# Hybrid attention and expert layer on one core: the end rebuilt, with weighted sums on TensorE and the last expert's tile added by a 0/1 matrix

## The chip, the cores and the metric

The kernel runs on one core of one Trainium2 chip. A core has five engines that work side by side: TensorE (PE in the profile; its weight loads are PEld), VectorE (DVE), ScalarE (ACT), GpSimd (POOL) and SyncE (SP), which here only issues transfers. They meet through semaphores. SBUF is the working memory with 128 partitions, PSUM the memory of 8 banks (512 f32 per partition each) into which TensorE writes. The metric is the device time of one execution in microseconds (us).

## The reference, cut to what matters

One layer on 128 context tokens (x_prompt) and 512 latent tokens (x_sample), width 1024: modulation from c, attention and a gated spatial mixer side by side, an output projection, then a mixture of 32 experts of which each token uses two. Around each half stands a norm, and its gated result is added to the residual. All of it is f32.

```python
x = x + gate1 * _rms_norm(mix, g_post_mix)
h2 = _rms_norm(x, g_pre_ffn) * (1 + scale2) + shift2
# _hier_moe: softmax over 4 groups, best group; in it the best two of 8 experts
weights = jax.nn.softmax(e_top, axis=-1) * g_top          # two weights per token
hid = silu(t @ w_gate[e]) * (t @ w_up[e])                 # per expert, 1024 -> 256
f = sum over the token's two experts of weight * (hid @ w_down[e])
x = x + gate2 * _rms_norm(f, g_post_ffn)                  # outputs y_prompt, y_sample
```

## The kernel before

The 640 tokens are 5 tiles of 128 (tile 0 is the context, cond_of(i) picks its gate). Each engine has its own program, written out by hand; the order of work is the order of the lines in it, and semaphores tie the programs together. No planner is at work.

**Up to the experts.** Modulation, input projection (L600, L619), spatial mixer, attention (20 steps of head pairs), output projection (L722) and, tile by tile beside it, residual, second norm and router. SP writes the gates to DRAM (L453) and reads them back broadcast (L455). After attention POOL reloads the residual into res (L1661, L1662). The router's result is turned into row numbers: src_row says which half rows of h2 an expert's tile gathers, dst_row where its results go. Two consecutive partition halves hold the two 512-wide halves of 64 rows (SLOT = 64), so one tile serves 64 assignments of an expert. Where an expert has more, extra tiles follow; extra_at[e] and extra_at[e+1] are the first and the end of expert e's extra tiles. With these inputs there are three.

**One expert e** (weights of 3 MB, six places: four ring slots, w_5, w_6):
- POOL gathers its rows from DRAM (gather), SP has loaded w_gate, w_up, w_down (load_expert, L436, L438).
- TensorE transposes them (next_x, L520), VectorE copies them to xt (copy_x, L1358).
- TensorE: products with w_gate and w_up (products, gate_up, L869), ScalarE SiLU (silu, L1572), VectorE times the up part (hidden, L1365).
- TensorE transposes hid (L520), ScalarE copies it (L1582), TensorE: product with w_down (down, L877), ScalarE copies the result to a y buffer (L1586), POOL scatters it to expert_results in DRAM (scatter, L1699). There are three y buffers.
- Then every engine loads extra_at[e] and extra_at[e+1] into registers and, if there are extra tiles, loops over them with the same weights (TensorE L914 to L926, VectorE L1374 to L1380, ScalarE L1587 to L1596, POOL extras, L1711). The loop waits for each step of its own tile.

Experts 0 to 25 run with the products of e+1 ahead of the down product of e. From expert 26 on (is_late, the part written out after the loop) an engine finishes e, its extra tiles included, and only then takes the next: TensorE does next_x(e+2), then products(e+1) (L928 to L931); VectorE copy_x(e+2), then hidden(e+1).

**The end.** SP waits for the scatters of all 32 experts and for the extra tiles' (L506, L507) and issues five reads of 1 MB, one per token tile: y_back[:, i] holds both experts' results of the 128 tokens. Per tile then: ScalarE y_sum = y_back[0] x w_tok[0] (L1606), VectorE y_sum += y_back[1] x w_tok[1] (L1397), ScalarE the squares with their sum (L1615), VectorE mean plus EPS (L1407), POOL to the power -1/2 (L1628), VectorE times that and the gate (L1410), VectorE plus residual (L1412), SP store (L513). VectorE's order is weighted(i+1), mean(i), then the last two steps of tile i-1:

```python
for i in range(TILES + 1):
    if i + 1 < TILES: weighted(i + 1)
    if i < TILES: ...          # waits for f_sq, mean of tile i
    if i: ...                  # waits for f_rs, the two last steps of tile i - 1
```

## Time and profile before

| | |
|---|---|
| median of 3 runs | 674.7 us (673.72 to 675.25) |
| the profiled execution's own time | 672.75 us |
| its span, first to last instruction | 671.0 us |
| PE busy | 548.3 us (82%) |
| DVE, ACT, POOL busy | 192.8, 151.3, 173.5 us |
| chain that ended last | PE 54%, DMA 26%, DVE 8%, ACT 4% |
| mean DMA rate over the span | 254 GB/s |

The page cuts the span into 40 slices of 16.8 us; a digit is the busy share in tenths:

```
PE   0479999999987789999997899789899998878788700
DMA  8999108054199300620044959999999999999183
```

Busy times are sums per engine. The chain is followed back from the last instruction, at each step to what released it, and so shows what sets the time; in the timeline the bracket behind a row is the engine's idle time ahead of it and what ended it. "issue" is time in which the engine waited for nothing that the profile shows. Times in the trace count from the start of the span.

### The profile page before, as it was taken

How to read it: one execution, taken by the hardware profiler on the slowest of the kernel's cores; microseconds unless marked ns; L12 is line 12 of the kernel's file. 1: busy time of each engine (PE TensorE's matmuls, PEld its weight loads, DVE VectorE, ACT ScalarE, POOL GpSimd, SP SyncE). 2: the span in 40 equal slices, each digit the busy share in tenths (PEclk: the TensorE clock that was granted, in tenths of full speed). 3: DMA queues.
4: the chain of work that ended last, by engine and by line, in shares of the span. 5: the costliest groups of instructions: out<-in, count | busy, mean ns of one | idle time of the engine just before them, and what ended most of it. 6: DMA issues, size and time to landing. Idle time of an engine off the chain costs nothing.

```text
span 671.0 us, 9726 instructions
## 1 busy us (share of the span) xinstructions
PE 548.3 (82%) x3055; PEld 301.5 (45%) x3056; DVE 192.8 (29%) x575; ACT 151.3 (23%) x375; POOL 173.5 (26%) x240
## 2 busy tenths in 40 slices
PE   0479999999987789999997789899998878788700
PEld 0235654444354455455554445455554444444300
DVE  1150312001367763244467102011111111111037
ACT  2630102002126663232221011111111111111142
POOL 1000000002513332143335423334332222221212
PEclk9999999999998999999998899999998898899955
DMA  8999108054199300620044959999999999999183
GB/s 254 401 404 397 65 1 312 1 193 183 37 312 409 124 2 1 219 95 31 33 166 143 409 220 407 395 392 408 405 395 401 402 404 393 406 403 395 47 327 157
DMA packets 53192, 170.23 MB, mean 254 GB/s; under 512 B 7660, under 2 KB 8340, under 8 KB 52256
## 3 DMA queue, kind: packets, MB, share of 16 engines
q1 hardware_dynamic: 46112, 155.45, 60.1%
q0 software_dynamic: 6752, 14.13, 5.9%
q8 instruction: 23, 0.38, 0.2%
q10 hardware_dynamic: 288, 0.13, 0.1%
q14 instruction: 17, 0.14, 0.1%
HBM read 163.23 MB, written 14.58 MB: 265 GB/s over the span
## 4 chain that ended last, share of the span: by engine, by line
PE 54%; DMA 26%; DVE 8%; ACT 4%; SPq 3%; issue 3%; PEld 1%; PEldq 0%; POOL 0%; ACTq 0%; POOLq 0%; DVEq 0%
DMA ring<-in_w_down_dram 12%; PE ps L722 10%; PE ps L619 10%; PE ps L869 8%; PE ps L600 5%; PE ps L520 5%; DMA w<-in_w_down_dram 5%; DMA ring<-in_w_mod_dram 4%; PE ps L877 4%; PE ps L601 3%; PE ps L699 2%; PE ps L539 2%; DMA ring<-in_w_up_dram 2%; ACT probs L1495 2%; DVE probs L1130 1%
## 5 line engine op out<-in xcount | busy, mean ns | idle before, releaser
L869 PE MATMUL ps<-ring,xt 128*64 128x256 f32 x768 | 97.3, 410 | 19.9 <-DMA ring<-in_w_up_dram 12.3
L869 PEld LDWEIGHTS ps<-ring,xt 128*64 128x64 f32 x768 | 64.7, 148 | 58.6 <-issue 36.6
L619 PE MATMUL ps<-ring,h_t 128*128 128x512 f32 x160 | 69.5, 594 | 0.0
L1365 DVE TENSOR_TENSOR hid<-act_g,ps 128x128 f32<-128x128 f32 x32 | 9.2, 287 | 185.7 <-ACT act_g L1572 185.7
L722 PE MATMUL ps<-ring,mix_t 128*128 128x512 f32 x120 | 53.6, 596 | 0.0
L1699 POOL DMA_INDIRECT expert_results<-y_sb,idx_out x32 | 32.7, 1023 | 58.3 <-ACT y_sb L1586 55.4
L619 PEld LDWEIGHTS ps<-ring,h_t 128*128 128x128 f32 x160 | 30.1, 190 | 37.6 <-issue 37.6
L869 PE MATMUL ps<-w,xt 128*64 128x256 f32 x352 | 40.4, 382 | 6.0 <-DMA w<-in_w_up_dram 4.1
L877 PE MATMUL ps<-ring,hid_t 128*64 128x512 f32 x176 | 42.6, 605 | 3.2 <-ACT hid_t L1582 2.6
L600 PE MATMUL ps<-ring,h_t 128*128 128x512 f32 x80 | 42.0, 607 | 2.7 <-DVE h_t L1022 2.7
L1628 POOL TENSOR_TENSOR gm_stats<-gm_stats,half_pow 128x8 f32<-128x8 f32 x5 | 9.7, 1939 | 129.5 <-DVE gm_stats L1088 129.5
L1688 POOL DMA_INDIRECT xg<-h_rows,idx_in x32 | 33.4, 1045 | 30.7 <-POOL idx_in L1685 24.3
L1572 ACT ACTIVATE act_g<-ps 128x128 f32<-128x128 f32 x32 | 8.9, 278 | 139.7 <-PE ps L869 139.7
L869 PEld LDWEIGHTS ps<-w,xt 128*64 128x64 f32 x352 | 27.8, 137 | 21.1 <-issue 12.0
L539 PE MATMUL ps<-ring,cond 128*32 128x384 f32 x256 | 23.9, 518 | 14.7 <-DMA ring<-in_w_mod_dram 14.7
L1656 POOL TENSOR_SCALAR probs<-probs,att_stats 128x384 f32<-128x384 f32 (+2 forms) x40 | 23.0, 589 | 48.1 <-DVE att_stats L1144 48.1
L1586 ACT COPY y_sb<-ps 128x512 f32<-128x512 f32 x32 | 18.8, 586 | 68.0 <-PE ps L877 68.0
L722 PEld LDWEIGHTS ps<-ring,mix_t 128*128 128x128 f32 x120 | 22.2, 190 | 25.8 <-issue 25.7
L1628 POOL TENSOR_TENSOR stats<-stats,half_pow 128x1 f32<-128x1 f32 (+1 forms) x16 | 13.4, 837 | 75.4 <-DVE stats L1188 39.5
L1358 DVE COPY xt<-ps 128x512 f32<-128x512 f32 x32 | 22.1, 691 | 22.7 <-PE ps L520 20.4
L520 PE MATMUL ps<-cst,probs 128*128 128x128 f32 x120 | 19.9, 289 | 10.4 <-ACT p_t L1505 9.0
L1685 POOL COPY idx_in<-src_row 128x1 uint32 (+1 forms) x29 | 6.5, 225 | 78.6 <-PE ps L520 78.5
(238 smaller groups left out, 725.5 us busy)
## 6 DMA issues: line engine op xcount, KB each, us to landing
ring<-in_w_mod_dram SPq DMA_DIRECT2D x8, 3072.0 KB, 20.2
ring<-in_w_gate_dram SPq DMA_DIRECT2D x22, 1024.0 KB, 9.3
ring<-in_w_up_dram SPq DMA_DIRECT2D x22, 1024.0 KB, 13.7
ring<-in_w_down_dram SPq DMA_DIRECT2D x22, 1024.0 KB, 16.0
w<-in_w_gate_dram SPq DMA_DIRECT2D x10, 1024.0 KB, 8.6
w<-in_w_up_dram SPq DMA_DIRECT2D x10, 1024.0 KB, 13.6
w<-in_w_down_dram SPq DMA_DIRECT2D x5, 1024.0 KB
w_6d<-in_w_down_dram SPq DMA_DIRECT2D x5, 1024.0 KB, 16.2
```

The costliest lines, as they stand in the source:

```text
L520: return pe.matmul(out, in_, ident[0:n_in, 0:n_in], is_transpose=True, start=True, stop=True)
L539: last = pe.matmul(ps[32 * g:32 * g + 32, hh, 0:MB // 2], cond[:, k, :], w[:, k, hh * (MB // 2):(hh + 1) * (MB // 2)], start=(k < 4), stop ...
L600: pe.matmul(ps[:, 4 + 2 * (i % 2), 0:ATT], h, w[:, k, 0:ATT], start=(k == 0), stop=(k == KC - 1))
L619: last = pe.matmul(ps[:, 4 + u % 4, :], h_t[:, k, i * P:(i + 1) * P], w[:, k, :], start=(k == 0), stop=(k == KC - 1))
L722: last = pe.matmul(ps[:, 2 * (i % 2) + hh, :], mix_t[:, k, i * P:(i + 1) * P], rhs, start=(k == 0), stop=(k == KC - 1))
L869: last = pe.matmul(bank[fh * SLOT:(fh + 1) * SLOT, 0:FE].rearrange("p (a f) -> p a f", a=2), x_t[:, k % 4, (k // 4) * SLOT:(k // 4 + 1) * ...
L877: last = pe.matmul(bank[ch * SLOT:(ch + 1) * SLOT, :], h[:, fh * SLOT:(fh + 1) * SLOT], w[:, fh, ch * 512:(ch + 1) * 512], start=(fh == 0) ...
L1358: dve.tensor_copy(xt[:, c % 2].rearrange("p c s -> p (c s)"), ps[:, c % 2, :]).then_inc(x_cp, 1)
L1628: pool.tensor_tensor(dst, src, half_pow[:, 0:n], ALU.pow).then_inc(done, 1)
L1656: last = pool.tensor_scalar(p, p, att_stats[:, INV, t, a:a + 1], 1.0, ALU.mult, ALU.mult)
L1688: pool.indirect_dma_start(xg[:, j, :], None, h2_halves, bass.IndirectOffsetOnAxis(ap=idx_in[:, j, 0:1], axis=0), bounds_check=2 * TILES * ...
L1699: pool.indirect_dma_start(y_halves, bass.IndirectOffsetOnAxis(ap=idx_out[:, c, 0:1], axis=0), y_buf(c), None, bounds_check=2 * TOPK * TILE ...
```

## The change

It has five parts.

1. **End.** The two weighted sums of a tile go to TensorE. w_diag[:, i, k] is the identity times w_tok (one 128x128 matrix per tile and choice), and per tile and 512-wide half three products add up in one PSUM bank: w_diag x y_back of choice 0, the same of choice 1, and sel_last x y_l, which adds the last expert's rows. ScalarE squares straight from PSUM, VectorE's step with the gate reads PSUM. y_back now lies in ring slots 2 and 3, y_out, junk_3 and gate_f where w_5 and w_6 were. Four pairs of banks turn; tile 4 waits for tile 0's output.
2. **Last expert (LAST = 31).** It isn't scattered. Its result is copied with a scale of w_last, the weight that belongs to each of its rows, and sel_last[:, i] has a 1 where a row of its tile belongs to a token of tile i. Since its rows of expert_results are read and never written now, SP zeroes all of expert_results in attention (five writes of 1 MB from a tile of zeros that POOL sets), and POOL's reload of the residual waits for them. w_last comes from a small table of weights in DRAM that POOL writes and gathers ahead of scatter 26. SP's wait before the five reads covers the scatters of experts 0 to 30 and the extra tiles'.
3. **Extra tiles of the last expert** are looked for after those of expert 30 and before the last expert's own products, on TensorE, VectorE and ScalarE; TensorE waits there for the last expert's weights.
4. **Late order.** From expert 26 on TensorE does products(e+1), then next_x(e+2), and VectorE hidden(e+1), then copy_x(e+2).
5. select_last() on VectorE makes w_diag and sel_last after the copy_x of expert 31, in expert 29's step; three small steps for w_pair and w_last follow the extra rows. Two semaphores (ws_raw and gmn_bc in, xg_x zeroed) are merged with others.

```diff
@@ sync: after the gates, and before the five reads @@
+            sp.wait_ge(zeros_made, 1)
+            for i in range(TILES):
+                sp.dma_start(y_dram[i * P:(i + 1) * P].rearrange("t k (h n) -> t (k h) n", n=512),
+                             zeros[:].unsqueeze(1).broadcast_to((P, 2 * TOPK, 512))).then_inc(s_gate, 16)
...
-            sp.wait_ge(rows_made, ALL_ROWS)
-            sp.dma_start(gate_bc[:, 1], gates_dram[1:2].broadcast_to((P, 2, D))).then_inc(gate_in, 16)
+            sp.wait_ge(y_mm, LAST - 1)
+            sp.wait_ge(expert_done, LAST - 1)
+            sp.dma_start(gate_f[:], gates_dram[1:2].broadcast_to((P, 2, D))).then_inc(gate_in, 16)
             for i in range(XS):
-                sp.wait_ge(y_st[i], 16 * len(range(i, EXPERTS, XS)))
+                sp.wait_ge(y_st[i], 16 * len(range(i, LAST, XS)))
...
@@ tensor, expert(q, c), after down(...) @@
+                if not below(e, LAST) and isinstance(e, int):
+                    return
+                extras(q, c, xb, e + 1)
+                pe.sem_inc(expert_done, 1)
+                if isinstance(e, int) and e + 1 == LAST:
+                    extras(*nth(q, c, 1), xb, LAST - 1)
+                if late and e + 1 < EXPERTS:
+                    products(*nth(q, c, 1))
+                if late and e + 2 < EXPERTS:
+                    next_x(*nth(q, c, 2))
+
+            def extras(q, c, xb, y_read):
+                e = q * WS + c
+                wgu, wd = weights(c)
+                if isinstance(e, int) and e == LAST:
+                    pe.wait_ge(wgu_in[c % LS], 32 * loads(q, c))
+                    pe.wait_ge(wd_in[c % LS], 16 * loads(q, c))
                 lo = pe.value_load(extra_at[0:1, bass.ds(e, 1)], min_val=0, max_val=MAX_EXTRA)
                 hi = pe.value_load(extra_at[0:1, bass.ds(e + 1, 1)], min_val=0, max_val=MAX_EXTRA)
                 with pe.If(lo < hi), pe.Fori(lo, hi) as x:
...
@@ tensor, after all_experts @@
+            y_l = y_buf(LAST % WS)
+            pe.wait_ge(y_cp, EXPERTS)
+            pe.wait_ge(rows_made, LAST_SEL)
+            for i in range(TILES):
+                pe.wait_ge(back_in[i], 16)
+                if i >= 4:
+                    pe.wait_ge(f_sq, i - 3)
+                    pe.wait_ge(f_out, i - 3)
+                for h in range(2):
+                    cut_, bank = slice(512 * h, 512 * (h + 1)), ps[:, 2 * (i % 4) + h, :]
+                    rows_ = slice(SLOT * h, SLOT * (h + 1))
+                    for k in range(TOPK):
+                        pe.matmul(bank, w_diag[:, i, k, :], y_back[:, i, k, cut_], start=(k == 0), stop=False)
+                    last = pe.matmul(bank, sel_last[rows_, i, :], y_l[rows_, :], start=False, stop=True)
+                last.then_inc(f_sum, 1)
...
@@ vector, expert(q, c) @@
+                extras(q, c, xb)
+                if isinstance(e, int) and e + 1 == LAST:
+                    extras(*nth(q, c, 1), xb)
+                if late and e + 1 < EXPERTS:
+                    hidden(*nth(q, c, 1))
+                if late and e + 2 < EXPERTS:
+                    copy_x(*nth(q, c, 2))
+                if isinstance(e, int) and e + 2 == LAST:
+                    select_last()
...
+            def select_last():
+                dve.tensor_copy(iota[:, 0:SLOT], const("slot")[:, 0:SLOT])
+                link(dve.tensor_scalar(iota[:, SLOT:P], const("slot")[:, 0:SLOT], float(SLOT), None, ALU.add))
+                link(dve.tensor_scalar(tok_l[:], dst_row[:, LAST:LAST + 1], 2, None, ALU.logical_shift_right))
+                link(dve.tensor_copy(tok_f[:, 0:1], tok_l[:]))
+                for i in range(1, TILES):
+                    last = dve.tensor_scalar(tok_f[:, i:i + 1], tok_f[:, 0:1], float(P * i), None, ALU.subtract)
+                link(last)
+                for i in range(TILES):
+                    for k in range(TOPK):
+                        dve.tensor_scalar(w_diag[:, i, k, :], ident, w_tok[:, i, k:k + 1], None, ALU.mult)
+                    last = dve.tensor_scalar(sel_last[:, i, :], iota[:], tok_f[:, i:i + 1], None, ALU.is_equal)
+                last.then_inc(rows_made, 1)
...
@@ vector, end: weighted(i) is gone, the rest keeps its order @@
+                    link(dve.scalar_tensor_tensor(y_out[:, i - 1].rearrange("p (h n) -> p h n", h=2), y_ps(i - 1),
+                                                  stats[:, 7, i - 1:i],
+                                                  gate_f[:, cond_of(i - 1), :].rearrange("p (h n) -> p h n", h=2),
+                                                  ALU.mult, ALU.mult))
+                    dve.tensor_tensor(y_out[:, i - 1], res[:, i - 1], y_out[:, i - 1], ALU.add).then_inc(f_out, 1)
...
@@ scalar, expert 31's copy @@
+                    act.wait_ge(wl_in, 16 + 16)
+                    act.activation(y_buf(c), ps[:, 5 + c % 2, :], ACT.Copy, scale=w_last[:, 0:1]).then_inc(y_cp, 1)
+                    return
...
@@ gpsimd, expert 26, ahead of its scatter @@
+                    pool.wait_ge(rows_made, WEIGHTS)
+                    pool.dma_start(w_dram.rearrange("(i p r) o -> p i (r o)", p=P, i=TILES),
+                                   w_pair[:].rearrange("p i k h -> p i (k h)")).then_inc(wl_in, 16)
+                    pool.tensor_copy(idx_l[:, 0:1], dst_row[:, LAST:LAST + 1]).then_inc(out_idx, 1)
+                    pool.wait_ge(wl_in, 16)
+                    pool.wait_ge(out_idx, e + 1)
+                    pool.indirect_dma_start(w_last[:, 0:1], None, w_dram,
+                                            bass.IndirectOffsetOnAxis(ap=idx_l[:, 0:1], axis=0),
+                                            bounds_check=2 * TOPK * TILES * P - 1, oob_is_err=False).then_inc(wl_in, 16)
```

## Rows read from the trace of the kernel before

**Rows 1.** Chain that ended last, 618 to 672 us: start, us, what
```profile
628.55 0.51 issue
629.06 3.69 PE ps L869 x32
...
636.09 0.59 ACT y_sb L1586
...
637.53 2.67 DMA expert_results<-y_sb,idx_out
...
641.11 8.91 DMA y_back<-expert_results
...
666.20 1.23 DVE y_out L1412
```

**Rows 2.** Timeline, experts 29 and 30: start, us, engine line op, idle before
```profile
612.38 3.67 PE L869 MATMUL ps<-ring,xt 128*64 128x256 f32 x32
...
616.41 0.29 DVE L1365 TENSOR_TENSOR hid<-act_g,ps 128x128 f32<-128x128 f32 x1 [3.23 <-ACT act_g L1572]
...
619.30 0.75 PE L520 MATMUL ps<-cst,xg_x 128*128 128x128 f32 x4
...
620.09 0.69 DVE L1378 COPY xt<-ps 128x512 f32<-128x512 f32 x1 [3.39 <-PE ps L520]
...
620.83 3.67 PE L869 MATMUL ps<-ring,xt 128*64 128x256 f32 x32 [0.78 <-DVE xt L1378]
```

**Rows 3.** Timeline of one issue on SP; DMA views of w_up's landings
```profile
597.89 0.46 SPq L436 DMA_DIRECT2D ring<-in_w_up_dram  x1
...
w<-in_w_up_dram SPq DMA_DIRECT2D x1, 1024.0 KB, 14.8
...
ring<-in_w_up_dram SPq DMA_DIRECT2D x1, 1024.0 KB, 13.1
```

**Rows 4.** DMA view, first 12 us: KB each, us to landing
```profile
v_all<-in_cache_v_dram POOLq DMA_DIRECT2D x1, 64.0 KB, 3.3
...
w_r<-in_router_group_dram POOLq DMA_DIRECT2D x1, 16.0 KB, 4.4
```

**Rows 5.** Chain, 40 to 50 us: VectorE steps
```profile
45.38 0.18 DVE pre L996
...
45.88 1.38 DVE h_t L1022 x5
```

**Rows 6.** Timeline of TensorE: gate and up products of three experts
```profile
508.83 5.36 PE L869 MATMUL ps<-ring,xt 128*64 128x256 f32 x32 [2.37 <-DMA ring<-in_w_up_dram]
...
551.46 3.67 PE L869 MATMUL ps<-w,xt 128*64 128x256 f32 x32 [2.34 <-DMA w<-in_w_up_dram]
...
576.88 5.36 PE L869 MATMUL ps<-ring,xt 128*64 128x256 f32 x32 [2.06 <-DMA ring<-in_w_up_dram]
```

**Rows 7.** Lines 914 and 927, 601 to 605 us: ns min/median/max, start
```profile
L914 PEldq TENSOR_LOAD <-extra_at x1: 314/314/314, 602.2 to 602.2; - x1
...
L927 PEldq EVENT_SEMAPHORE  x1: 51/51/51, 603.8 to 603.8; - x1
```

**Rows 8.** Chain, 100 to 160 us; groups by form of weight loads
```profile
113.40 27.47 PE ps L619 x64
...
L619 PEld LDWEIGHTS ps<-ring,h_t 128*128 128x128 f32 x160 | 30.1, 190 | 37.6 <-issue 37.6
```

**Rows 9.** Timeline of the end
```profile
640.26 2.56 SPq L509 DMA_DIRECT2D y_back<-expert_results  x5
645.08 1.15 ACT L1606 ACTIVATE y_sum<-y_back,w_tok 128x1024 f32<-128x1024 f32 x1 [8.40 <-DMA y_back<-expert_results]
...
659.97 1.06 ACT L1615 ACTIVATE junk<-y_sum 128x1024 f32<-128x1024 f32 x1 [2.29 <-DVE y_sum L1397]
...
662.37 0.14 DVE L1407 TENSOR_SCALAR stats<-stats 128x1 f32<-128x1 f32 x1
```

**Rows 10.** Windows, attention: engines' busy us, clock, DMA share, GB/s
```profile
230.00:240.00 10.00, 8.75 (x69) 5.19 (x65) 6.81 (x27) 4.78 (x15) 2.73 (x4) 1.00 0.00 0
```

More of the change, by code:

```diff
@@ L48 @@
 LOOPED = (EXPERTS - 2 - WS) // WS
+LAST = EXPERTS - 1
 MB = 768
@@ L1596, in expert @@
                     act.copy(y_x[:, :], ps[:, 5 + c % 2, :]).then_inc(e_yc, 1)
-                if late and e + 1 < EXPERTS:
-                    silu(*nth(q, c, 1))
             silu(0, 0)
@@ L1647, in _ @@
                     pool.tensor_tensor(gm_v[:, i - 1], gm_v[:, i - 1], gmn_bc[:], ALU.mult).then_inc(gv_ready, 1)
+            pool.wait_ge(gm_tr, TILES)
+            pool.memset(zeros[:], 0.0).then_inc(zeros_made, 1)
             INV = 6
@@ L1748, in expert @@
                     gather_ahead(*nth(q, c, 2))
+                if isinstance(e, int) and e == 2 + LOOPED * WS:
+                    pool.wait_ge(rows_made, WEIGHTS)
[7 more added lines that the diff above has]
+                                            bounds_check=2 * TOPK * TILES * P - 1, oob_is_err=False).then_inc(wl_in, 16)
+                if not below(e, LAST) and isinstance(e, int):
+                    extras(e)
+                    return
                 scatter(q, c)
```

91 lines of the change are left out of this document (48 added, 43 removed).

## Prediction, made before the changed kernel ran

> **What bounds the kernel now.** I read the page's slices, then the chain that ended last, then the timeline of its last 60 us. Weights stream at 400 GB/s from about 400 us on; the page's DMA slices are full there, and until 577 us the chain runs through them. From 576.88 us [rows 6] it runs through TensorE alone: expert 26 to 31 follow one another at 7.6 to 7.8 us, every step waiting for the one before. At 619.30 us expert 30's extra tile starts, and it costs a whole round: transposes, VectorE's copy, gate and up products at 620.83 [rows 2], y_x copied and free at 628.55, and only then expert 31's products at 629.06 [rows 1]. Its result is copied until 636.68 (636.09 + 0.59), scattered (2.67), read back (first tile used at 645.08, 4.82 after its issue at 640.26 [rows 9]), and from there on VectorE is the bound: 3.7 us a tile, last step from 666.20 to 667.43, then the store, until the span ends at 671.0. What has to be compared is one stretch: from the copy of expert 31's result at 636.68 to 671.0, 34.3 us. The profiled execution took 672.75 us, 1.75 more than its span and 1.95 less than the median of 674.7; I work on the span and add 3.70 at the end.
>
> **Early parts, at nothing.** The zeros (five writes of 1 MB) go out after the gates' write, in a stretch where the DMA engines stand still: share 0.00 from 230 to 240 us [rows 10], and so to 265; 5 MB at 400 GB/s is 13 us, and the residual's reload, which now waits for them, was issued at 269 us anyway. If they overran, the reload and with it all of the router would be late by the overrun. On POOL the memset of zeros lies in a gap of 16 us before its first probabilities. One semaphore for ws_raw and gmn_bc joins two loads that both land long before use. The three small VectorE steps after the extra rows fall in its wait of 3.3 us for expert 1's SiLU.
>
> **POOL at expert 26.** The weights' write (640 pieces of 16 B) and the gather of w_last now stand ahead of scatter 26, gather 31 and scatter 27. POOL will stand 6 to 8 us for the landing. Gather 31 then lands near 606 us and is wanted at 615, buffer y of expert 26 is wanted again at 611: covered by 5 us or more. The pieces do take DMA time from a full stream: 1024 pieces of 16 B landed 1.1 us later than 128 larger ones [rows 4], so 0.7 us here, bounds 0 and 1.5.
>
> **Late experts: products ahead of the next transposes.** The four transposes (0.72 us) move into the 0.70 us in which TensorE waits for SiLU and the product. Four experts (26 to 29) could give 2.7 us. But the weights of expert 30 arrive late: w_up is issued at 597.89, and these issues land 13.1 to 14.8 us later [rows 3], at 611.0 to 612.7, plus the pieces above. Its products stood at 612.38 [rows 2], so what remains is 0 to 1.1 us; I take 0.4. Call the new start U, 612.0.
>
> **select_last() on VectorE.** It stands after copy_x of expert 31 and ahead of the copy of the extra tile. Products of expert 30 take 3.67; hidden ends at U+4.3 (616.41+0.29 against 612.38); copy_x, whose transposes now come after the products, runs to U+5.15. Then one copy, three linked small steps at 0.21 and four tiny ones with a link: 1.3 us [rows 5]. Then 15 steps of 128x128 f32 out of SBUF; five such took 1.38, 0.276 each, but with two column operands, and with one a bit less: I take 0.24, so 3.6 us, bounds 2.2 and 4.2. It ends at U+10.1. Then come the two loads of extra_at and the branch on VectorE's sequencer, 1.3 us, of which I take 0.6 hidden. The extra's copy can start at U+10.8. It is wanted at U+7.7 (620.09 against 612.38 [rows 2]). So the extra tile is 3.1 us late, bounds 0 and 4.5.
> By the Trainium skill (TensorE: Matmul & The Clock Gate, section on the array's architectural detail) VectorE's queue takes eight instructions ahead in order; the whole check would then lie beside the last selection steps, and the delay would be 2.4, the sum 0.7 smaller. No row here shows how far its sequencer runs ahead.
> TensorE then stands 0.78 + 3.1 us before the extra's products. After 2.06 and 2.37 us of standing such a group took 5.36 instead of 3.67; after 2.34 once 3.67 [rows 6]. The page shows 6.09 us of L869 in the chain where expert 0's extra tile had waited. I take 1.9 more, bounds 0 and 2.4.
>
> **extras() of expert 31 ahead of its products.** Expert 31 has no extra tile (three in all: one at expert 0, one near 418 us, one at expert 30), but the check is made: two loads of extra_at and a branch on TensorE's sequencer. From the first load to the next semaphore step it is 602.2 to 603.8, 1.6 us [rows 7]. Elsewhere this lies under the down products; here it comes after the wait for y_x, where before 0.51 us stood [rows 1], and nothing covers it. With two more waits, 1.7 us. TensorE has then stood since 627.83 for 1.23 + 1.7 = 2.9 us, longer than any group that kept its speed [rows 6], so the products take 1.7 more; bounds 0 and 1.7.
>
> **The end.** The result of expert 31 is ready (636.68 before) at 636.68 − 0.4 + 3.1 + 1.9 + 1.7 + 1.7 = 644.7. Its scatter is gone, 2.67 and the issue. The return is no longer on the path: it waits for the extra's scatter, issued at 629.76 before, hence 634.5 now; with 2.5 to land, some 0.4 for POOL's check and 4.8 to the first tile [rows 9] it is there at about 642.2.
> The sums: 5 tiles x 2 halves x 3 products of 512 columns in f32. The input projection streams such products back to back, 64 records and two to a product: 27.47 / 32 = 0.858 us each [rows 8]. 30 x 0.858 + 0.2 to fill = 25.9 us. The selecting product has half the rows, but a product's time goes by its columns, and between two of them stand full ones. Weight loads, 60 at 0.19, are inside that pitch [rows 8].
> The Trainium skill (the same page, The mechanism) says that weight loads lie beside running products only for other row groups. By it 60 x 0.19 = 11.4 us would come on top and the sum would be 21 instead of 9.6; the row, with full rows loading beside full rows at the bare pitch, speaks against it, and I leave it no chance.
> 5.15 us a tile is more than VectorE's 3.7, so the last sum ends at 644.7 + 25.9 = 670.6. Behind it: the squares with their accumulator 1.15 [rows 9], 0.1 to VectorE, and then the old tail. VectorE's order is kept (mean of tile 4, then the two steps of tile 3, then those of tile 4), so from the mean at 662.37 to the span's end at 671.0 it is 8.63 as before [rows 9], plus 0.15 as one operand is now in PSUM. 10.0 in all: 680.6.
> **Sum on the span:** 680.6 − 671.0 = +9.6. By terms: scatter and return gone, TensorE's sums and tail in their place, 25.9 + 10.0 − 34.3 = +1.6; order −0.4; selection +3.1; clock +1.9; check +1.7; clock +1.7. Time 682.4 against 672.75, and 684.3 against the median.
>
> **Rivals.**
> A. The selection is done in time (steps of 0.1 us, or queued so that the copy slips in): no 3.1 and no 1.9, +4.6, 679.3. For it: VectorE is nearly idle there. Against it: [rows 5], even at the low bound of 2.2 us it ends after U+7.7.
> B. The clock holds at both places: 9.6 − 3.6 = +6.0, 680.7. For it is 551.46 [rows 6], against it the two others.
> C. Faster: a product with a 0/1 or diagonal matrix takes one record, 0.43 us, not two. Place: the 30 sums. Price: 30 x 0.43 = 12.9 instead of 25.7, so −3.2, 671.5. It decides below 0.858 − (9.6 + 1.35)/30 = 0.49 us a product. For it: the program's transposes, products with a constant matrix, do take one record each. Against it: those are transposes; every plain f32 product has two records [rows 8].
> D. The order gains its whole 2.7, the selection is in time and the clock holds: 1.6 − 2.7 + 1.7 = +0.6, 675.3, no change. Against it is the landing of w_up [rows 3].
> That the change doesn't do what it says: if the return were still held by a late scatter it would show first at 642.2 + 2.5, which TensorE's own lateness hides.
>
> **Chances.** Forecast 0.48, A 0.20, B 0.14, C 0.10, D 0.08. A measurement of this kernel tells 0.2%, 1.35 us, from no change. Slower 0.82 (forecast, A, B), same 0.08 (D), faster 0.10 (C). The range reaches from D's 675 up to 688 (delay and clock at their upper bounds, +1.4 and +0.5, no gain by order, +0.4, and 1.4 for the piece writes and PSUM operands); C is left out.
>
> **What would show it.** On the timeline: 15 VectorE steps between copy_x of expert 31 and the extra's copy, and the idle time of TensorE ahead of it (near 3.9 us); groups of L869-like products above 5 us for the extra tile and for expert 31; idle of 2.9 us before the latter; first sum about 0.7 us after the last down product; 5.15 us between sums; last sum to end of span 10 us; return landed ahead of TensorE. I am wrong if the sums are paced at 2.5 us by the landing, if the extra's copy comes within 1 us of its transposes, or if the end from expert 31's copy on is under 34 us.

## The result, and the profile after

The changed kernel takes 684.56 us (median of 4, 682.05 to 686.67) against 674.98 for the kernel before (median of 4): ratio 1.0149, 95% interval 1.0119 to 1.018. It is slower by 9.6 us, and 684.3 us was predicted. That the total agrees to 0.3 us is partly luck: of the terms that it was added up from, two were 1.75 and 1.9 us too large, two 3.8 and 1.2 us too small, and these errors largely cancelled.

The profiled execution took 686.67 us with a span of 684.9, 13.9 more than the span before. That is more than the medians differ, and the surplus lies ahead of everything the change is about: expert 26's products begin at 579.88 instead of 576.88 [rows 6]. From there to the end of the span it is 105.0 us against 94.1 (671.0 − 576.88), so 10.9 more. Every comparison below counts from that point; whether this is fair is the question of the last two experiments.

Timeline of the kernel after, expert 30, its extra tile, expert 31 (start, us, engine line op, names, shapes; in the bracket the engine's idle time ahead of it and what ended it). It answers to [rows 2]:
```profile
615.39 3.67 PE L889 MATMUL ps<-ring,xt 128*64 128x256 f32 x32 [0.28 <-DMA ring<-in_w_up_dram]
...
619.78 0.69 DVE L1409 COPY xt<-ps 128x512 f32<-128x512 f32 x1
...
620.39 0.18 DVE L1448 COPY iota<-cst 128x64 f32<-128x64 f32 x1
...
624.25 0.28 DVE L1458 TENSOR_SCALAR sel_last<-iota,tok_f 128x128 f32<-128x128 f32 x1
624.45 0.68 DVE L1443 COPY xt<-ps 128x512 f32<-128x512 f32 x1
...
625.18 3.67 PE L889 MATMUL ps<-ring,xt 128*64 128x256 f32 x32 [2.12 <-DVE xt L1443]
...
632.30 0.59 ACT L1677 COPY y_x<-ps 128x512 f32<-128x512 f32 x1 [2.11 <-PE ps L897]
...
635.17 6.57 PE L889 MATMUL ps<-ring,xt 128*64 128x256 f32 x32 [2.99 <-issue]
```
Between VectorE's copy for expert 31 (619.78) and the copy of the extra tile (624.45) stand the selection's steps, 620.39 to 624.53. The extra tile's products begin 9.79 us behind those of expert 30; before it was 8.45 (620.83 − 612.38 [rows 2]): 1.35 more. They keep their speed (3.67). Then y_x is free at 632.89, and TensorE begins expert 31 at 635.17, idle for 2.99; and these products take 6.57 us.

The chain that ended last, which answers to [rows 1] and [rows 3] (start, us, what):
```profile
601.13 14.22 DMA ring<-in_w_up_dram
...
632.89 2.28 issue
...
645.84 1.98 PE ps L986 x4
```
The 0.51 "issue" of [rows 1] is 2.28 now: the check for extra tiles of expert 31. The scatter and the return have gone from the chain, as the change meant. Products of expert 30 wait for w_up, issued at 601.13 and landed 14.22 us later.

The end, answering to [rows 9], and TensorE's groups from 645 to 676 us (columns of a group: count, busy us, mean ns of one record; two records are one product):
```profile
636.61 2.50 SPq L529 DMA_DIRECT2D y_back<-expert_results  x5
...
645.10 0.69 ACT L1657 ACTIVATE y_sb<-ps,w_last 128x512 f32<-128x512 f32 x1 [2.04 <-PE ps L897]
...
647.75 1.12 PE L987 MATMUL ps<-y_sb,sel_last 64*128 64x512 f32 x2
...
647.75 0.29 PEld L987 LDWEIGHTS ps<-y_sb,sel_last 64*128 64x128 f32 x2 [0.76 <-issue]
...
648.80 0.30 PEld L986 LDWEIGHTS ps<-y_back,w_diag 128*128 128x128 f32 x2 [0.76 <-issue]
...
674.45 1.12 PE L987 MATMUL ps<-y_sb,sel_last 64*128 64x512 f32 x2
675.61 1.02 ACT L1687 ACTIVATE junk<-ps 128x1024 f32<-128x1024 f32 x1 [4.82 <-PE ps L987]
...
676.76 0.15 DVE L1474 TENSOR_SCALAR stats<-stats 128x1 f32<-128x1 f32 x1 [3.33 <-ACT junk L1687]
...
680.59 1.23 DVE L1481 TENSOR_TENSOR y_out<-res,y_out 128x1024 f32<-128x1024 f32 x1
...
L986 PE MATMUL ps<-y_back,w_diag 128*128 128x512 f32 x40 | 19.8, 618 | 0.8 <-ACT y_sb L1657 0.8
L987 PE MATMUL ps<-y_sb,sel_last 64*128 64x512 f32 x20 | 11.2, 641 | 0.0
```
The return is issued at 636.61 and is no longer waited for. The sums begin 0.05 us behind the copy (645.84) and the last ends at 675.57: 29.7 us for 30 products, 5.9 a tile. Between a diagonal product and a selecting one, in either direction (647.75 and 648.80), weight loads show an idle time of 0.76 us; inside a pair of diagonal products they follow at 0.24. The granted clock is 1.00 all through these sums, so the clock has no part in their pace. From the last sum to the end of the span it is 9.3 us.

The zeros, answering to [rows 10] (busy us of each engine, clock, DMA share, GB/s):
```profile
230.00:240.00 10.00, 7.91 (x62) 4.98 (x64) 6.93 (x27) 6.94 (x22) 4.61 (x7) 1.00 1.05 407
```
They fill the DMA engines in this stretch, where they stood still, and nothing waited for them: the next issue on SP, st_bc's, came 3.56 us later than before (280.72 against 277.16), POOL's reload of the residual, which does wait for them, 3.57 later (272.67 against 269.10), and the offset had that size, within 0.1, at 219 us already, ahead of the first write of zeros at 225.53.

### The profile page after: what moved, and what is told of

Its sections match the earlier page's. It is cut to its first block, busy times and chain, and to the rows that moved or that the text cites. A ratio compares the mean times of both kernels' runs of the same rounds, so it can differ in the third digit from the quotient of the medians.

```text
span 684.9 us, 9871 instructions
## 1 busy us (share of the span) xinstructions
PE 583.9 (85%) x3115; PEld 313.1 (46%) x3116; DVE 190.7 (28%) x596; ACT 145.9 (21%) x370; POOL 171.6 (25%) x242
## 4 chain that ended last, share of the span: by engine, by line
PE 51%; DMA 31%; DVE 6%; ACT 3%; issue 3%; SPq 3%; PEld 1%; POOL 1%; PEldq 0%; DVEq 0%; ACTq 0%; POOLq 0%
DMA ring<-in_w_down_dram 16%; PE ps L742 10%; PE ps L639 10%; DMA w<-in_w_down_dram 7%; PE ps L620 5%; PE ps L540 5%; DMA ring<-in_w_up_dram 4%; PE ps L889 3%; PE ps L559 3%; PE ps L986 3%; PE ps L621 3%; DMA ring<-in_w_mod_dram 2%; PE ps L719 2%; ACT probs L1564 2%; PE ps L987 2%
## 5 line engine op out<-in xcount | busy, mean ns | idle before, releaser
L889 PE MATMUL ps<-w,xt 128*64 128x256 f32 x352 | 42.1, 393 | 9.0 <-DMA w<-in_w_up_dram 7.3
L639 PEld LDWEIGHTS ps<-ring,h_t 128*128 128x128 f32 x160 | 30.1, 190 | 37.6 <-issue 37.6
L1701 POOL TENSOR_TENSOR stats<-stats,half_pow 128x1 f32<-128x1 f32 (+1 forms) x16 | 9.5, 595 | 97.5 <-DVE stats L1236 39.8
L621 PEld LDWEIGHTS ps<-ring,h_t 128*128 128x128 f32 x80 | 15.8, 197 | 20.3 <-issue 20.3
```

Source lines behind the costliest of these rows:

```text
L621: last = pe.matmul(ps[:, 5 + 2 * (i % 2), 0:2 * KVW], h, w[:, k, ATT:QKV], start=(k == 0), stop=(k == KC - 1))
L639: last = pe.matmul(ps[:, 4 + u % 4, :], h_t[:, k, i * P:(i + 1) * P], w[:, k, :], start=(k == 0), stop=(k == KC - 1))
L889: last = pe.matmul(bank[fh * SLOT:(fh + 1) * SLOT, 0:FE].rearrange("p (a f) -> p a f", a=2), x_t[:, k % 4, (k // 4) * SLOT:(k // 4 + 1) * ...
```

## The experiments

All are the changed kernel with one edit, unless said otherwise. Each ratio is to runs of the kernel before made in the same batch (median 673.99 us for e1 to e4, 674.31 for e5 to e8, 675.19 for e9 to e11), so medians of different batches may differ by some 1 us without a cause in the kernel. Beside times I give five stretches of the profiled execution, since single terms of 1 to 3 us are near what the medians can tell (their intervals reach 1.3 to 2.8 us to each side):

```
                       exp. 26  30 to   extra   31 to   copy
                       to 30    extra   to 31   copy    to end  total
before                 35.50    8.45    8.23    7.03    34.91    94.1
before, second trace   35.50    8.46    8.22    7.04    34.90    94.1
after                  35.51    9.79    9.99    9.93    39.80   105.0
after, second trace    35.32    9.80    9.95    9.97    39.81   104.9
e1 selection early     35.43    9.98   10.00    8.72    39.77   103.9
e2 no check of 31      35.38   11.48    8.23    7.03    40.12   102.2
e3 pairs               35.17    9.78   11.60    7.03    33.60    97.2
e4 old order           35.54    8.99   10.01    8.71    39.82   103.1
e5 full rows           35.50    9.79    9.90    8.51    36.08    99.8
e6 loads ahead         36.05    9.76    8.70    7.04    39.77   101.3
e7 one choice          35.49    8.77   10.00    8.72    29.63    92.6
e8 together            34.90    9.16    8.61    7.04    29.89    89.6
e9 one tile both       35.66    9.19    8.62    7.03    28.69    89.2
```
The stretches lie between the starts of the products of expert 26, 30, the extra tile and expert 31, the start of the copy of its result, and the end of the span.

**e1_select_early.** The selection two steps earlier.
```diff
-                if isinstance(e, int) and e + 2 == LAST:
+                if isinstance(e, int) and e + 4 == LAST:
                     select_last()
```


> The changed kernel with select_last() moved two experts earlier on VectorE (after copy_x of expert 29), nothing else. Theory T (the changed kernel's trace as read): the extra tile of expert 30 waits 1.35 us for VectorE (its copy starts 9.1 us after expert 30's products, 7.7 without the selection), the products behind it kept the clock, so 1.3 us less than the changed kernel, about 683.2 against 684.6, and in the profile the extra's copy comes within 0.1 us of its transposes. Theory P (the prediction as written): 3.1 us plus 1.9 us of clock, so 5 us less, 679.6. Rival R: nothing changes, since a gain at the extra tile is lost again to the clock or to the weights.


Measured: 682.03 us median (6 runs; 680.75 to 685.9), ratio to before 1.0112 (1.0074 to 1.015). Timeline of TensorE:
```profile
615.63 5.19 PE L889 MATMUL ps<-ring,xt 128*64 128x256 f32 x32 [2.61 <-DMA ring<-in_w_up_dram]
...
625.61 3.67 PE L889 MATMUL ps<-ring,xt 128*64 128x256 f32 x32 [0.78 <-DVE xt L1443]
...
635.61 5.36 PE L889 MATMUL ps<-ring,xt 128*64 128x256 f32 x32 [3.00 <-issue]
```
The wait for the extra's copy is back at the 0.78 of [rows 2], so the selection was the whole of that delay. Here the clock fell at expert 30 instead (5.19), so the 9.98 us from there are 1.52 slow products and 8.46 of old length. Expert 31's products took 5.36 instead of 6.57. So the trace is 1.1 us shorter in all, and this is the clock at expert 31: the 1.35 won ahead of the extra tile went to the clock at expert 30. The median fell by 2.5; the two intervals overlap.

**e2_no_check31.** TensorE's check for extra tiles of expert 31 is left out (such tiles would not be computed).
```diff
-                if isinstance(e, int) and e + 1 == LAST:
-                    extras(*nth(q, c, 1), xb, LAST - 1)
```


> The changed kernel without TensorE's look for extra tiles of expert 31 (this leaves out extra tiles of the last expert on TensorE, of which these inputs have none). Theory T: between y_x free and expert 31's products 2.28 us stand, 0.51 without the check; TensorE then idles 1.2 instead of 3.0 us, the products take 3.67 instead of 6.57 us: 1.8 + 2.9 = 4.7 us less, 679.9. Theory P: 1.7 + 1.7 = 3.4 us less, 681.2. Rival R (the time goes with the wait for expert 31's weights, not with the check): no change, the idle time stays near 3 us and would be put down to a DMA.


Measured: 684.48 us median (6 runs; 679.78 to 686.02), ratio 1.0131 (1.009 to 1.0172): the times can't tell it from the changed kernel. The trace can:
```profile
617.44 5.36 PE L889 MATMUL ps<-ring,xt 128*64 128x256 f32 x32 [2.55 <-DMA ring<-in_w_up_dram]
...
637.15 3.67 PE L889 MATMUL ps<-ring,xt 128*64 128x256 f32 x32 [1.24 <-ACT y_x L1675]
```
Expert 31 starts 8.23 us behind the extra tile and runs at 3.67, as before: 1.76 and 2.90 gained, 4.66 in all. 1.69 is given back by a clock fall at expert 30, 0.3 by the first tile's sums, which now wait for y_back. The median shows none of the remaining 2.8 us, but 2.8 less than 684.56, a ratio of 1.0115, lies within its interval: the times neither confirm nor exclude it. The edit takes out the waits for expert 31's weights too, but these are not what cost the time: in the changed kernel the DMA engines stand still from 632.20 to 635.10 us (share 0.00), so the weights had landed.

**e3_pairs.** All diagonal products of a tile first, then its two selecting products.
```diff
-                for h in range(2):
-                    for k in range(TOPK): pe.matmul(bank, w_diag[:, i, k, :], ...)
-                    last = pe.matmul(bank, sel_last[rows_, i, :], ...)
+                for k in range(TOPK):
+                    for h in range(2): pe.matmul(banks[h], w_diag[:, i, k, :], ...)
+                for h in range(2): last = pe.matmul(banks[h], sel_last[rows_, i, :], ...)
```


> The changed kernel with the sums of a tile in another order: the four diagonal products of both halves first, then the two 64-row selecting products side by side (rows 0 to 63 and 64 to 127). Theory S (a change between 128-row and 64-row operands costs about 0.2 us, because the next weights are not loaded beside the running product; 5.93 us a tile instead of 5.15): two changes a tile instead of four and the two selecting products overlapped: 4 x 0.858 + 0.9 + 0.4 = 4.7 us a tile, 6 us less in all, 678.5. Rival L (each 64-row product takes 1.05 us by itself and each 128-row pair 1.91, whatever the order): 5.93 less at most one overlapped product, 5.0 us a tile, 4.6 us less, 680; if 64-row products don't overlap either: 5.9 us a tile and no gain.


Measured: 677.86 us median (12 runs; 675.5 to 681.74), ratio 1.0059 (1.0034 to 1.0084); 6.7 under the changed kernel, 6.1 by the two ratios.
```profile
642.74 3.70 PE L985 MATMUL ps<-y_back,w_diag 128*128 128x512 f32 x8 [0.79 <-ACT y_sb L1659]
646.37 1.13 PE L989 MATMUL ps<-y_sb,sel_last 64*128 64x512 f32 x4
647.43 3.70 PE L985 MATMUL ps<-y_back,w_diag 128*128 128x512 f32 x8
```
A tile takes 4.69 us instead of 5.93. The two 64-row products (four records) take 1.13 together, where one alone took 1.12: with their operands on different halves of the 128 rows they ran side by side. So the gain of 1.24 a tile is two changes fewer (0.4) and the time of one product (0.86). The rival, by which a pair of diagonal products takes 1.91 us whatever the order, would make four of them 3.82 us; they take 3.63 (642.74 to 646.37), which is 4 x 0.858 and one change. The end is 6.2 us shorter. In this trace the clock fell at the extra tile (5.36) and, for once, not at expert 31, although TensorE stood 2.92 us ahead of it.

**e4_old_order.** Next transposes ahead of the products again, and VectorE's two steps likewise.
```diff
-                if late and e + 1 < EXPERTS: products(*nth(q, c, 1))
                 if late and e + 2 < EXPERTS: next_x(*nth(q, c, 2))
+                if late and e + 1 < EXPERTS: products(*nth(q, c, 1))
```


> The changed kernel with the late order as before the change (from expert 26 on the transposes of e+2 ahead of the products of e+1, on VectorE the copy ahead of hidden). Theory T: the weights of expert 30 set the start of its products at about the same moment in either order, so the order is worth 0 to 0.4 us: 684.6 to 685. Theory P: 0.4 us, the same within noise. Rival O: the new order gains its full 0.7 us in four experts, and undoing it costs 2.7 us, 687.3; a second rival: without it TensorE stands less long before the products of experts 29 and 30, keeps its clock there, and the old order is faster by up to 1.7 us.


Measured: 684.47 us median (6 runs; 682.98 to 687.24), ratio 1.0147 (1.0109 to 1.0184), the same as with the new order. From expert 26 to 30 it is 35.54 against 35.51, for two different reasons. With the old order TensorE's own work fills the stretch, and the products of expert 30 wait for nothing. With the new one experts 27 to 29 follow faster (in e1 at 7.10 and 6.90 us from start to start, here at 7.75 and 7.64), and TensorE then waits for w_up: 2.61 us in e1; in the changed kernel 2.04 at expert 29, whose products then ran slow, and 0.28 at expert 30. The issue of w_up stands 21.0 us behind the start of expert 26's products in both e1 and e4, and in e1 it lands 14.4 us later, so the time won is waited away. And the extra tile comes 0.54 late instead of 1.35, because in the old order the copy for expert 31, and so the selection, begins earlier. The median is the same although the trace is 1.9 us shorter (0.8 at the extra tile, 1.2 at expert 31, whose products took 5.36); the interval covers that too:
```profile
626.96 3.67 PE L889 MATMUL ps<-ring,xt 128*64 128x256 f32 x32 [1.32 <-DVE xt L1443]
```

**e5_full_rows.** The selecting products take all 128 rows; the other half's rows are added too, so the result is not the layer's, and only the time counts.
```diff
-                    last = pe.matmul(bank, sel_last[rows_, i, :], y_l[rows_, :], ...)
+                    last = pe.matmul(bank, sel_last[:, i, :], y_l, ...)
```


> The changed kernel, with one edit: each selecting product takes all 128 rows of sel_last and of the last tile instead of the 64 that belong to its half (so the last expert's contribution to the sums is wrong: the other half is added as well). Order and number of products stay as in the changed kernel. Theory S (what the end pays above 30 x 0.858 us is paid at each change between 128-row and 64-row operands, 20 of them at about 0.2 us): with one shape only, a tile takes 6 x 0.858 = 5.15 us instead of 5.93, the end is 3.9 us shorter, 680.7 us in all. Rival T (the selecting product is slow for what it reads or for the change of weights' source): a tile stays at 5.9 us, 684.6 us. Rival U (the cost lies at the change of bank, with which each half begins): also 5.9 us a tile, as the order of banks is the same; e3_pairs had more changes of bank and was shorter, which speaks against it.


Measured: 680.34 us median (6 runs; 678.53 to 683.0), ratio 1.0084 (1.0056 to 1.0113); 4.2 under the changed kernel where 3.9 was expected.
```profile
646.24 1.88 PE L986 MATMUL ps<-y_back,w_diag 128*128 128x512 f32 x4
...
647.96 1.02 PE L987 MATMUL ps<-y_sb,sel_last 128*128 128x512 f32 x2
...
648.82 1.88 PE L986 MATMUL ps<-y_back,w_diag 128*128 128x512 f32 x4
```
A half begins every 2.58 us (646.24, 648.82), which is 3 x 0.86, the pace of [rows 8], with the same order of banks and the same number of products. Twice the rows cost nothing; the changes of shape, two per half, cost 0.39 of the 2.97 us that a half took. The end is 3.7 us shorter; the rest of the trace's 5.2 is expert 31, whose products took 5.16.

**e6_loads_ahead.** The two registers of expert 31's check are loaded before expert 30's down products; compare and branch stay.
```diff
+                if isinstance(e, int) and e + 1 == LAST:
+                    seen_ = [pe.value_load(extra_at[0:1, bass.ds(e + 1 + n, 1)], ...) for n in range(2)]
                 pe.wait_ge(ht2_cp, e + 1)
```


> The changed kernel, with one edit: TensorE loads the two registers of the last expert's check before expert 30's down products, where it waits for ScalarE anyway; only the compare and the branch stay behind the copy of the extra tile's result. If the two loads are the larger part of the 1.77 us that the check adds between that copy and the products of expert 31 (2.28 us now, 0.51 before), this stretch falls to 1.0 to 1.4 us. If the branch (a jump, and its target's instructions) is the larger part, it stays at 1.8 to 2.3 us. Time about 683.7 us by the first, 684.6 by the second; a single look can't tell these, the stretch in the trace does.


Measured: 683.37 us (one run, from which the gain can't be told; the trace shows it).
```profile
633.21 0.59 ACT L1680 COPY y_x<-ps 128x512 f32<-128x512 f32 x1 [2.11 <-PE ps L897]
...
634.79 3.67 PE L889 MATMUL ps<-ring,xt 128*64 128x256 f32 x32 [1.71 <-ACT y_x L1680]
```
y_x is free at 633.80, expert 31 begins 0.99 later, instead of 2.28: the loads were 1.3 of the 1.77. With 1.71 us of idle time its products take 3.67, not 6.57. By its stretches the edit is worth 4.2 us, most of it clock; 0.5 was lost ahead of expert 30, at w_up.

**e7_one_choice.** The sum shared between engines.
```diff
-                    for k in range(TOPK):
-                        pe.matmul(bank, w_diag[:, i, k, :], y_back[:, i, k, cut_], start=(k == 0), stop=False)
+                for h in range(2):
+                    pe.matmul(banks[h], w_diag[:, i, 0, :], y_back[:, i, 0, 512 * h:512 * (h + 1)], start=True, ...)
...
+                dve.scalar_tensor_tensor(y_out[:, i], y_back[:, i, 1], w_tok[:, i, 1:2],
+                                         y_ps(i), ALU.mult, ALU.add).then_inc(f_sum, 1)
```


> The changed kernel, with the sum shared: TensorE makes only the first choice's weighted product and the selecting product of each half (four products a tile, the two of one shape side by side), VectorE adds the second choice with one operation per tile, reading the banks, into y_out, and ScalarE squares that; five of the fifteen matrices of the selection fall away. Theory (the change's own idea, that the scatter and its return leave the path, is worth some 6 us, and is lost because TensorE sums at 5.93 us a tile where VectorE needed 3.6): the first tile's four products end 2.9 us behind the copy of the last result, at 648.8 in the changed kernel's trace, VectorE then needs 21.1 us as before and the store 3.6, which ends at 673.5 instead of 684.9, 11.4 us less: 673 us in all, 2 us under the kernel before. Rival (VectorE's operations on the banks are slower than on SBUF, or VectorE and ScalarE hold each other up at the banks): 1.5 us a tile is lost again, 680 us. Rival (TensorE stays the bound, at a low clock): 4.6 us a tile or more, 679 us or more.


Measured: 673.75 us median (12 runs; 671.44 to 675.57), ratio 0.9986 (0.9967 to 1.0005): not to be told from the kernel before.
```profile
642.80 1.98 PE L984 MATMUL ps<-y_back,w_diag 128*128 128x512 f32 x4 [0.79 <-ACT y_sb L1665]
...
644.72 1.13 PE L988 MATMUL ps<-y_sb,sel_last 64*128 64x512 f32 x4
...
645.98 1.28 DVE L1473 SCALAR_TENSOR_TENSOR y_out<-y_back,w_tok,ps 128x1024 f32<-128x1024 f32 x1 [6.63 <-PE ps L988]
...
655.55 1.27 DVE L1473 SCALAR_TENSOR_TENSOR y_out<-y_back,w_tok,ps 128x1024 f32<-128x1024 f32 x1
...
659.26 1.27 DVE L1473 SCALAR_TENSOR_TENSOR y_out<-y_back,w_tok,ps 128x1024 f32<-128x1024 f32 x1
```
TensorE needs 2.97 us a tile, VectorE 3.71 (655.55 to 659.26). Its operation that reads the banks takes 1.28, like the old one on SBUF. By the stretches the end is 10.2 us shorter than in the changed kernel, and 5.3 shorter than before.

**e8_together.** e7 with the edits of e1 and e6.


> e7_one_choice with two more edits: the selection built two steps earlier (as in e1_select_early) and the registers of the last check loaded ahead (as in e6_loads_ahead). By the sum of its parts: 673.2 - 0.9 (what is left of the selection's delay with ten matrices) - 1.0 (loads) = 671.3 us, about 3.5 us under the kernel before (0.995). Rival: what is gained ahead of the end is taken back by the return of y_back, which lands only about 1 us before it is needed, or by the clock behind TensorE's idle time: 673 us, as e7_one_choice.


Measured: 671.24 us median (12 runs; 668.8 to 673.89), ratio 0.9947 (0.9927 to 0.9967). TensorE's idle time ahead of expert 31 is 1.62 us and the clock stays.

**e9_one_tile_both.** e8; for the last tile TensorE makes both weighted products.
```diff
-                    pe.matmul(banks[h], w_diag[:, i, 0, :], ...)
+                for k in range(TOPK if i == BOTH else 1):
+                    for h in range(2): pe.matmul(banks[h], w_diag[:, i, k, :], ...)
```


> e8_together with one more edit: of the last of the five tiles TensorE makes both weighted products (six products, the two selecting ones behind the four others), so that VectorE has no addition for it, and ScalarE squares it in the banks. If VectorE alone sets the end of e8_together (three operations of 1.28, 1.27 and 1.23 us a tile, no idle time from 652.8 us on in its trace), the end comes one operation earlier, 1.2 us: 670.0 us, 4.3 us under the kernel before (0.9935). TensorE ends that tile about 656.6 us in that time frame, where VectorE's addition had begun at 656.51, so it has to be in time for the square. Rival (TensorE's longer tile or the square's wait takes its place): 671.2 us, the same as e8_together.


Measured: 669.42 us median (6 runs; 667.11 to 671.76), ratio 0.9906 (0.9873 to 0.9938); 5.8 us under the kernel before. The last steps:
```profile
653.96 3.70 PE L989 MATMUL ps<-y_back,w_diag 128*128 128x512 f32 x8
...
658.76 1.02 ACT L1707 ACTIVATE junk<-ps 128x1024 f32<-128x1024 f32 x1 [1.49 <-PE ps L993]
...
661.10 1.27 DVE L1493 SCALAR_TENSOR_TENSOR y_out<-y_out,stats,gate_f 128x1024 f32<-128x1024 f32 x1
...
664.86 1.23 DVE L1497 TENSOR_TENSOR y_out<-res,y_out 128x1024 f32<-128x1024 f32 x1
```
VectorE has no addition for the last tile, and the end comes 1.20 us earlier (28.69 against 29.89), as worked out.

**e10_before_again and e11_after_again.** Both kernels unchanged, for second traces.


> The kernel before, once more, for a second trace. In the traces so far the products of expert 26 began at 576.9 us in the kernel before and at 578.4 to 582.4 us in nine traces of changed kernels, which do the same work up to there but for 5 writes of zeros, one small write and one small read. Theory V (the offset is spread between executions, from the clock at the start and in attention): the second trace of the kernel before has it anywhere from 576 to 582 us, span and offset moving together. Rival W (the change costs 1.5 us or more ahead of expert 26, in its writes of zeros or its 20 KB of pair weights): it is at 577 us again, within 0.5.

> The changed kernel, once more, for a second trace. Theory V: expert 26's products begin anywhere from 577 to 582 us. What the prediction put to the clock (products 3.67 or 5.36 us, 6.57 once, behind 2.0 to 3.0 us without a product) is expected to fall out differently at one or more of the four places where it can (experts 26 and 30, the extra tile, expert 31), as idle times of the same length have gone either way; if it is the same at all four as in the first trace (3.67 at 26, 5.36 at 29, 3.67 at the extra tile, 6.57 at 31), the clock follows from the kernel's order rather than from the execution.


Measured: 676.6 and 684.83 us. The kernel before, second trace, and then the changed one:
```profile
580.68 5.36 PE L869 MATMUL ps<-ring,xt 128*64 128x256 f32 x32 [2.08 <-DMA ring<-in_w_up_dram]
...
624.64 3.67 PE L869 MATMUL ps<-ring,xt 128*64 128x256 f32 x32 [0.78 <-DVE xt L1378]
...
632.86 3.67 PE L869 MATMUL ps<-ring,xt 128*64 128x256 f32 x32 [1.23 <-ACT y_x L1596]
```
```profile
578.25 3.67 PE L889 MATMUL ps<-ring,xt 128*64 128x256 f32 x32 [0.36 <-DMA ring<-in_w_up_dram]
...
613.57 3.67 PE L889 MATMUL ps<-ring,xt 128*64 128x256 f32 x32 [2.15 <-DMA ring<-in_w_up_dram]
...
623.37 3.67 PE L889 MATMUL ps<-ring,xt 128*64 128x256 f32 x32 [2.12 <-DVE xt L1443]
...
633.32 6.61 PE L889 MATMUL ps<-ring,xt 128*64 128x256 f32 x32 [2.96 <-issue]
```
The kernel before now stands at 580.68 where it stood at 576.88, and the changed one at 578.25: most of the offset ahead of expert 26 belongs to the execution. A mean cost of about 1 us there isn't excluded: the two traces of before stand at 578.8 in the mean, the eleven of changed kernels at 580.0. Behind expert 26 both kernels repeat within 0.2 us: 94.1 and 94.1, 105.0 and 104.9. The clock did not differ at any of the four places where the expectation looked for it (3.67 at experts 26 and 30 and the extra tile, 6.57 and 6.61 at expert 31). It differs at expert 29 (5.36 and 3.67), but there the idle times differ too (2.04 and 1.15). Further ahead the same place, behind the same idle time, went both ways; first the first trace of the changed kernel, then the second:
```profile
511.45 5.30 PE L889 MATMUL ps<-ring,xt 128*64 128x256 f32 x32 [2.19 <-DMA ring<-in_w_up_dram]
```
```profile
510.01 3.67 PE L889 MATMUL ps<-ring,xt 128*64 128x256 f32 x32 [2.21 <-DMA ring<-in_w_up_dram]
```

## Why the prediction was right in sum, and where not in its parts

Against the 94.1 us of before, per term (predicted, then measured in both traces of after):

```
selection delays the extra tile   +3.1   +1.35
clock at the extra tile           +1.9    0
check of expert 31                +1.7   +1.77
clock at expert 31                +1.7   +2.9
late order                        -0.4    0
copy with scale                    0     +0.1
end from the copy's end           +1.6   +4.8
total                             +9.6  +10.9
```
The last term is 39.1 us (684.9 − 645.79) against the 34.3 of [rows 1]. The 10.9 of the traces and the 9.6 of the medians (interval 8.0 to 12.1) agree. The mechanisms that were named are mostly there, but the sizes are not: the errors of the terms add up to over 8 us if their signs are left out, and to 1.3 us with them. The agreement of the total is to that extent luck.

**Scatter and return off the path: right.** They are gone from the chain, the return is issued 8.5 us ahead of the last copy (636.61, 645.10) instead of 4.2 behind it (640.26 [rows 9], 636.09 [rows 1]). e7 shows that this saving is real: with the old pace of 3.7 us a tile restored, the end is 5.3 us shorter than before (29.63 against 34.91).

**"30 x 0.858 + 0.2 to fill = 25.9 us" for the sums: the step that failed most, 29.7.** The pace of [rows 8] is right for products of one shape (e5 runs at it). The step "a product's time goes by its columns, and between two of them stand full ones" left out that the operands change between 128 and 64 rows 20 times. At each change the next weights come 0.76 us behind the last ones instead of 0.24, and about 0.2 us are lost, 3.9 in all. By this e3 (fewer changes) should shorten the end by 6.2 us and e5 (none) by 3.9; they did so by 6.2 and 3.7. That the time is lost at the change and not inside the 64-row product shows in both neighbours: a pair of diagonal products ahead of a change takes 1.91 us (645.84 to 647.75) instead of 1.72, the selecting product ahead of the next one 1.05 (to 648.80) instead of 0.86. The Trainium skill (TensorEngine Tiling (Array Packing), Key Properties) says that "Mode switching requires drain": I had not weighed it. The trace agrees that a change costs time, 0.2 us each; that a drain is the reason, no run shows. The rule that the prediction weighed and gave no chance, of the Trainium skill (TensorE: Matmul & The Clock Gate, The mechanism), that weight loads lie beside products only for other row groups, is not borne out among products with full rows: in e5 the loads of 0.19 lie in a pitch of 0.86.

**Selection: mechanism right, size 3.1 for 1.35.** The terms were 3.6 us for fifteen steps and 0.6 for the check behind them. The steps follow at 0.20 us (620.39 to 624.53 for all, 4.1 against 4.9), and the check took nothing: the copy starts at 624.45, before the last step's end. The Trainium skill (TensorE: Matmul & The Clock Gate, section on the array's architectural detail) gives VectorE's queue eight instructions in order, by which the check would lie wholly beside the selection; the trace agrees. e1 takes the term away entirely. Of the 1.35 us that were left, 0.8 came from the late order: with the old one (e4) it is 0.54.

**Late order: worth nothing, in place of −0.4.** With the new order the landing of w_up sets the stretch to expert 30, and with the old one TensorE arrives at the same moment (e4). Nothing either from the write and gather of pair weights that can be told: the stretch from expert 26 to 30 is 35.45 in the mean of the eleven traces with them (34.90 to 36.05) and 35.50 without.

**Check: right (1.7, measured 1.77), shown by e2 and split by e6** into 1.3 for the loads and 0.5 for the rest (the two waits, the compare and the branch).

**Clock: right that it would cost, wrong in place and size.** At the extra tile TensorE stood 2.12 us, not 3.9, and kept its speed in both traces, though not in e3 (2.11, 5.36). At expert 31 it stood 2.99 us, and nearly the whole group ran at the lower of the two levels, 1.2 GHz. The clock had already fallen within the idle time ahead of it (windows of the kernel after; engines' busy us, granted clock, DMA share, GB/s):
```profile
625.20:628.90 3.70, 3.65 (x32) 2.19 (x32) 0.00 (x0) 0.00 (x0) 1.16 (x2) 1.00 0.35 131
632.20:635.10 2.90, 0.00 (x0) 0.00 (x0) 0.00 (x0) 0.59 (x1) 1.16 (x2) 0.85 0.00 0
635.20:641.70 6.50, 6.50 (x32) 3.84 (x32) 0.00 (x0) 0.00 (x0) 0.00 (x0) 0.55 0.64 237
```
The upper bound of 1.7 came from [rows 6], where a group lost at most that; 2.9 lay outside it. The prediction held a nearer row, the 6.09 us of expert 0's extra tile (2.4 more), and used it as a bound for the other place only. In all 13 traces together, of the experts' groups of 32 products from 410 us on, none behind an idle time under 1.9 us was slow (of 209 that show one), of those behind 1.97 to 2.66 us 54 of 82 were, and of those behind 2.9 to 3.0 us six of seven (5.16, three times 5.36, 6.57, 6.61). The seventh, e3's, had kept its speed behind 2.92 us, and there the group just before it had been slow. Left out of this count is expert 0's extra tile, near 381 us: its group took 5.36 to 6.62 us in all 13 traces with only 0.78 us directly ahead of it, but TensorE had stood 2.5 to 3.4 us just before the four transposes in front.

**Tail: 10.0, measured 9.3.** VectorE's steps on the banks took 1.27 and 1.28, as on SBUF, so the extra 0.15 did not come; the way from the last sum to the mean was 1.19 instead of 1.25; and from VectorE's last step to the span's end it was 3.1 us (681.82 to 684.9), before 3.6 (667.43 to 671.0).

Of the rivals, A (selection in time) was half true, and B (the clock holds) was true at the extra tile and not at expert 31. Rival C is refuted: two records a product, as in [rows 8]. Rival D, whose order gains 2.7 us, is refuted by e4. What stays open: what decides the clock after 2 to 3 us without products (3.67, 5.19 and 5.36 all occur), and whether e2 and e4 are faster than the changed kernel by the 2.8 and 1.9 us of their traces, which their medians don't show and their intervals allow.

## What to carry to other kernels

Taking a transfer off the path only pays if the work put in its place keeps the pace of what it replaces: here the 5.3 us that scatter and return are worth (e7 against before) became a loss of 4.9 at the end, because TensorE alone made the sums at 5.9 us a tile. Dividing them so that no engine needs more than 3.7 took the 1.5% loss away (e7), and with the two edits ahead of the end and one tile shared differently it became a gain of 0.9% (e9). Put products of one shape together; a change between 128 and 64 rows cost 0.2 us each time. A check that never fires costs its register loads where nothing covers them, and through TensorE's idle time it can cost more again in clock (here 1.8 us, and up to 2.9 for the clock); load its registers where the engine waits anyway.

## What the runs showed of the hardware that was not expected

- Two 64-row products on the two halves of the rows took 1.13 us together, one alone 1.12 (e3 against after).
- The clock behind an idle time of about 2 us is no constant of the kernel: the same place of the changed kernel came out at 5.30 (511.45, behind 2.19) and at 3.67 (510.01 in the second trace, behind 2.21), and expert 26, up to which the changed kernel, e1, e5 and e6 run the same program, at 3.67, 5.36, 5.36 and 5.36, each behind 2.06. Idle times of 2.9 to 3.0 us ahead of expert 31 cost up to 2.9 us.
- Two executions of one kernel differed by 3.8 us ahead of expert 26 (576.88 and 580.68, the kernel before) and by 1.6 (579.88 and 578.25, the changed one), while the stretch behind that point repeats within 0.2: a single trace is best compared from a point just ahead of the change.
- Small VectorE steps of 128x128 f32 without a link between them follow one another at 0.20 us, though each shows 0.28.
